# Value products of an attention layer written as two 64-column halves of TensorE's array

## What is computed

```python
scores = einsum('bnqhgd,bnkhd->bnhgqk', q, kb) * (HEAD_DIM ** -0.5)   # kb, vb: previous and own block of 128 keys
scores = where(valid, scores - slopes * dist, NEG)
p = softmax(concatenate([scores, sink_col], -1))[..., :-1]
o = einsum('bnhgqk,bnkhd->bnqhgd', p, vb).reshape(B, S, BRANCH)       # the value products
...
y = (o * silu(z)) @ w_out
x = x + rmsnorm(y, g_post)
```

## Time and profile before

| | us |
|---|---|
| median of 3 runs | 2489.99 |
| lowest and highest | 2487.33, 2490.1 |
| span of the profiled execution | 2484.1 |
| PE busy in it | 2415.9 (97%) |
| DVE busy | 1100.6 (44%) |
| ACT busy | 759.7 (31%) |

### The profile page before, as it was taken

One profiled execution on the slowest core, in us unless ns is written; L12 is line 12 of the kernel. 1 busy time (PEld: TensorE's weight loads), 2 busy tenths in 40 slices (PEclk: granted clock), 3 DMA queues, 4 the chain that ended last, 5 costly groups with the idle time before them and its releaser, 6 DMA issues.

```text
span 2484.1 us, 28260 instructions
## 1 busy us (share of the span) xinstructions
PE 2415.9 (97%) x10534; PEld 1909.7 (77%) x10534; DVE 1100.6 (44%) x1410; ACT 759.7 (31%) x1190; POOL 258.7 (10%) x221
## 2 busy tenths in 40 slices
PE   7999999999999999999999999999999999999995
PEld 6777777777888688877777778868888777777884
DVE  7555655556225433334444442262433444445123
ACT  5332333334222331232323242233222332324221
POOL 3100000001113300000000021151000000001113
PEclk9998999999999999999999999999999999999998
DMA  7211111113224322212121142271222212213321
GB/s 281 92 51 68 65 54 68 68 51 127 111 101 183 144 97 102 87 64 87 57 75 55 68 155 100 84 271 68 102 86 82 75 56 83 72 57 119 118 101 68
DMA packets 36357, 238.95 MB, mean 96 GB/s; under 512 B 4160, under 2 KB 4416, under 8 KB 11840
## 3 DMA queue, kind: packets, MB, share of 16 engines
q1 hardware_dynamic: 29520, 204.47, 22.7%
q10 hardware_dynamic: 6336, 25.17, 2.6%
q0 software_dynamic: 432, 8.39, 0.8%
HBM read 221.24 MB, written 16.78 MB: 96 GB/s over the span
## 4 chain that ended last, share of the span: by engine, by line
PE 91%; DVE 4%; issue 2%; DMA 2%; ACT 1%; POOL 0%; ACTq 0%; SPq 0%; DVEq 0%; POOLq 0%
PE acc L444 71%; PE sc L444 4%; PE ov L711 2%; PE ov L543 2%; PE sc L597 2%; PE sc L520 2%; PE sc L519 2%; PE sc L700 1%; PE sc L692 1%; DMA xr<-residual 1%; PE sc L531 1%; DVE g L1086 1%; PE ov L444 1%; PE sc L691 1%; DMA g<-xT_dram 1%
## 5 line engine op out<-in xcount | busy, mean ns | idle before, releaser
L444 PE MATMUL acc<-h_hi,hi 128*128 128x512 f32 x2560 | 1027.6, 401 | 27.4 <-DVE h_lo L1111 15.1
L444 PE MATMUL acc<-h_lo,hi 128*128 128x512 f32 x2560 | 1005.9, 393 | 0.0
L444 PE MATMUL acc<-h_hi,lo 128*128 128x512 f32 x2560 | 1005.7, 393 | 0.0
L1054 DVE TENSOR_TENSOR lo<-raw,hi 128x2048 fp32r<-128x2048 f32 x175 | 388.9, 2222 | 566.0 <-ACT hi L748 563.7
L444 PEld LDWEIGHTS acc<-h_hi,hi 128*128 128x128 f32 x2560 | 486.6, 190 | 141.3 <-issue 23.1
L444 PEld LDWEIGHTS acc<-h_lo,hi 128*128 128x128 f32 x2560 | 487.2, 190 | 103.1 <-issue 5.3
L444 PEld LDWEIGHTS acc<-h_hi,lo 128*128 128x128 f32 x2560 | 486.3, 190 | 104.0
L748 ACT ACTIVATE hi<-raw 128x2048 fp32r<-128x2048 f32 (+2 forms) x178 | 330.7, 1858 | 162.6 <-PE acc L444 157.0
L755 ACT ACTIVATE sq<-acc 128x512 f32<-128x512 f32 x60 | 35.9, 599 | 470.9 <-PE acc L444 470.9
L331 POOL TENSOR_TENSOR sqacc<-sqacc,sq 128x512 f32<-128x512 f32 x74 | 102.3, 1382 | 450.0 <-ACT sq L755 448.2
L408 POOL TENSOR_TENSOR lo<-raw,hi 128x2048 fp32r<-128x2048 f32 x3 | 23.7, 7885 | 1040.0 <-ACT hi L748 1040.0
(11 more groups left out here) (197 smaller groups left out, 2198.8 us busy)
## 6 DMA issues: line engine op xcount, KB each, us to landing
raw<-w_dram SPq DMA_DIRECT2D x162, 1024.0 KB, 4.6
raw_m<-wm_dram SPq DMA_DIRECT2D x16, 1024.0 KB, 6.3
xr<-residual ACTq DMA_DIRECT2D x16, 512.0 KB, 6.0
residual<-g ACTq DMA_DIRECT2D x16, 512.0 KB, 6.0
raw<-w_dram SPq DMA_DIRECT2D x8, 896.0 KB, 4.3
g<-xT_dram SPq DMA_DIRECT2D x4, 1024.0 KB, 12.0
residual<-g POOLq DMA_DIRECT2D x1, 4096.0 KB, 13.8
area<-memT_dram POOLq DMA_DIRECT2D x2, 2048.0 KB, 11.6
```

The lines of the kernel that those rows point to most:

```text
L444: ins = pe.matmul(to, a, b, start=first and n == 0, stop=last and n == 2)
L1054: dve.tensor_tensor(lo[c.slot][:, 0:width], raw[c.slot][:, 0:width], hi[c.slot][:, 0:width].bitcast(F32), ALU.subtract).then_inc(lo_done, 1)
```

## The change

The two heads' products are no longer made one after the other over the array's full width. For each key block, the product of head 0 uses the first 64 columns of `vcur`'s block and writes partitions 0 to 63 of `ov[0]`; directly behind it the product of head 1 uses the other 64 columns and writes partitions 64 to 127 of `ov[1]`. `HALVES` is the pair of slices 0 to 63 and 64 to 127, and `HD` is 64. The loops over heads and key blocks change places.

```diff
-                for par in range(2):
-                    for kb in range(TB):
-                        n = 256 if kb < TB - 1 else P
+                for kb in range(TB):
+                    n = 256 if kb < TB - 1 else P
+                    for par, rows_ in enumerate(HALVES):
                         src = kb * 512 + par * 256
-                        ins = pe.matmul(ov[par][:, kb * P:kb * P + n], vcur[:, tile(kb, P)], pt1[:, src:src + n],
-                                        start=kb == 0, stop=kb == TB - 1, skip_group_check=True)
+                        ins = pe.matmul(ov[par][rows_, kb * P:kb * P + n], vcur[:, kb * P + par * HD:kb * P + (par + 1) * HD],
+                                        pt1[:, src:src + n], start=kb == 0, stop=kb == TB - 1, skip_group_check=True)
                 ins.then_inc(values1, 1)
```

## The result

The changed kernel takes 2515.9 us (2513.9 to 2516.3 in 4 runs), the kernel before 2488.7 us beside it. The ratio is 1.0116, with a 95% interval of 1.0102 to 1.0131. The profiled execution has a span of 2513.8 us against 2484.1.

The account below looks back on a forecast made before the run. PE was taken as the bound, with DVE's chain to the scores almost equally long. Span 2484.1 + 19.0 (clock) - 1.1 (pair 14) = 2502.0, plus 5.9 outside the span, gave 2508 us; range 2486 to 2527.

Parts of the forecast that it names:

- The overlap: Value products: the two heads run together in array halves, more than half overlapped, saving 0.8 to 1.5 us a pair.
- the changes of shape: Value products: PE goes from full array to halves and back, costing 0.2 to 0.4 us a pair, at most 1.7.
- The wait: Ahead of the first score: PE idles 0.9 to 1.2 us for L1201, so pairs 0 to 13 gain nothing.
- Pair 14's gain: Values between `z_a` and `z_b`, no scores close behind: about 1.1 us stays saved.
- pair 15's: Last pair's value products: nothing saved, since PE's next wait is for a tile of `h_lo` on DVE.
- The clock: 13 pair-loop turns: each gets a doubled lapse and takes 34.50 us, +19.0 us; with all at 34.74, +22.1.
- the double turn at 539.16: Turn with two blocks of scores, already at clock 0.96: left unchanged.
- What lies around the span: Outside the profiled span: a run takes 5.9 us more, 2490.0 against 2484.1.
- The argument on the clock: At the scores: a thin stretch grown from 5.0 to 6.1 us, emptier, leaves less room to escape a lapse.
- Lapses as they were: Rival, pair-loop turns: full clock lost as often as before, about 2489 us; chance 0.16.
- fewer lapses: Rival, pair-loop turns: more scores escape the clock's fall, 2477 us, or 2466 with the whole streaming gain; chance 0.13.
- No overlap: Rival, value products: 2.95 us stays and 0.2 to 0.4 for shape comes on top, say 2500 us; chance 0.18.

Follow-up runs that it names:

- grouped scores: Eight 128-row score products, then eight 64-row: kernel before 2416.0 us, changed kernel 2414.7; with scores before k-tile 3 as well, 2415.6 and 2399.5.
- the scores later: Scores placed before k-tile 3 of the gate chunk instead of k-tile 1: changed kernel 2487.9 us, kernel before 2498.0 us.
- the heads outside: Changed kernel with the old loop order, heads outside key blocks: 2524.3 us; with scores before k-tile 3 as well, 2508.1 us.
- the fastest kernel: Changed kernel with scores ordered 128-row products first, then 64-row, and placed before k-tile 3: 2399.5 us.

## Why the prediction was right, and where it was off

**The overlap: right.** Streaming was to save 0.8 to 1.5 us a pair and the changes of shape to take 0.2 to 0.4 of it, so that 1.9 us would be left of 2.95. Measured are 1.66, with the way back in them, and 0.09 more ahead, since the first matmul of the block starts 0.32 us behind its forerunner where 0.23 is usual: 1.75 us, a net saving of 1.20. A step from one half to the other costs nothing that shows (6 or 7 ns), which excludes the prediction's upper bound of 1.7 us. The Trainium skill ("TensorEngine Tiling (Array Packing)", Key Properties) says that tiles of one mode work in parallel, and the 16 matmuls in 1.66 us agree.

**The wait: right, with its size.** Predicted 0.9 to 1.2 us in each turn for L1201 and 3.8 us to the first score; measured 1.2 us, 14 times (the fifteenth wait listed is pair 0's 0.8, there before), and 3.87. Pair 14's gain was put at 1.1 us and measured 1.2; pair 15's was nothing, and went into a new wait for a tile of `h_lo`:

```profile
625.97 0.50 PE L444 MATMUL acc<-h_hi,hi 128*128 128x512 f32 x1 [1.18 <-DVE h_lo L1225]
```

**The clock: right in kind, too small in size.** This is the term that failed. I priced each turn at 34.50 us, the least of the four dearest turns of before, for +19.0 us. The turns took 456.2 / 13 = 35.1 us, +26.7. Of the 7.7 us between, 6.4 come from four turns with a lapse longer than any in the trace of before (0.86 at 36.1 us), and 1.3 from nine that took 34.65 on average. My upper bound of 34.74 a turn was taken from the rows, but nothing said that the worst row seen was the worst possible. The lapse was also placed wrongly, directly behind the scores, while the long ones begin inside them. I left the double turn at 539.16 as it was as well, since it stood at 0.96; it took 3.1 us more. Put right, these two make 2484.1 + 26.7 + 3.1 - 1.2 = 2512.7, against 2513.8.

**What lies around the span.** I took 5.9 us from the median's distance to the span. The profiled run of the changed kernel took 2515.8 us at a span of 2513.8, and the runs of before whose spans are on record lie 2.0 us above them too. So the profiled execution of before was one of about 2486.1 us, 3.9 us faster than the median of that time. That error went against the other: without it the forecast would have been 2504, and 12 us short in place of 8. That it came as near as it did is in part luck.

**The argument on the clock** was that a stretch that is thinner for longer leaves less room for turns without a lapse. The grouped scores and the doubled products support it. The runs with the scores later do not fit it alone: 2498 us for the kernel before, with nothing waited for, and half of the added lapses left in the changed kernel without its wait. The lapses depend on wait, scores and rhythm together, and I can't say from these runs how. That the forecast's direction came out rests on the part that was shown.

**The rivals.** Lapses as they were, and fewer lapses: refuted by the stretches. No overlap: refuted by the first timeline. The gain of the overlap was real, 1.20 us a pair on PE. Behind the moved scores it shortened a turn without a lapse, but there the lapses took it back (ratio 1.0001); only with the scores grouped and moved did 0.93 us a turn reach the end.

## What to carry to other kernels

Before making a stretch of TensorE faster, look at what the next stretch waits for: if another engine's chain ends as late, the saving becomes idle time, and it must be filled with work that is ready (here: six gate matmuls) to be worth anything, and even then the clock can take the gain back. Idle time next to matmuls that are thinly spaced isn't free: look at the granted clock turn by turn, not at its mean over the span. The larger prize lay in the thin stretch itself, matmuls of two shapes in alternation, and putting like shapes together gave 2.9% for a new order of the same products.

## What the runs showed of the hardware that was not expected

Two matmuls over 64 of the 128 rows, on different halves and into different banks, overlap as those on half the columns do: the eight `k_lo` products of the grouped scores start in twos, 1 to 4 ns apart, and take 0.67 us in the fastest kernel, 0.08 us each, where the same size follows each 0.12 us at full shape and took 0.31 in alternation:

```profile
218.45 1.21 PE L521 MATMUL sc<-k_hi,q 128*128 128x256 f32 x8
219.59 0.74 PE L523 MATMUL sc<-k_lo,q 64*128 64x256 f32 x8
220.27 0.50 PE L444 MATMUL acc<-h_hi,hi 128*128 128x512 f32 x1
```

Half of the value products taken out made the kernel before 32 us slower, and the half-column products issued twice made the changed kernel 24 us faster than once. A stretch whose clock lapses can reward work that does nothing.

How long a lapse lasts goes with the place where it begins. In the traces with the scores in alternation, the lapses that begin up to 2.3 us after the first score last 10.2 us, those from 2.4 to about 4.4 us after it 6.8 us, and those that begin later 3.4 us. Every lapse of 10.2 us stands at scores with a wait of 0.4 us or more ahead of them. Why, no run shows.

Turns can fall into a fixed rhythm with the lapses: 34.13 to 34.25 us again and again with the heads outside and the scores before k-tile 3, 31.64 and 33.2 in alternation before. The same scores, moved by six matmuls, made the kernel before 12 us slower.
